# A hybrid attention and retention step on one core: sampled values' products one pair later, the last gate's first two pairs in one group, sampled output turned in parts

## What is computed

```python
u = rms_norm(h, g_pre)
z = einsum('bsd,de->bse', u, w_in)             # 22528 columns: q, k, v, gates of both branches
ya = dilated window attention(q, k, v) * silu(za)      # 3 groups of 8 heads, head size 128
yr = retention(q, k, v, state), normed * g_ret * silu(zr)   # 8 heads, 256 x 256 state
merged = sigmoid(ga) * (ya @ w_a_out) + sigmoid(gb) * (yr @ w_r_out)
h = h + rms_norm(merged @ w_o, g_post)
h = h + sigmoid(h @ w_ple_gate) * (p @ w_ple_proj)
```

## Time and profile before

| | |
|---|---|
| median of 3 runs | 2968.15 us (2966.22 to 2971.32) |
| profiled execution, its own time | 2968.77 us |
| its span, first to last instruction | 2967.0 us |
| mean granted TensorE clock | 0.99 |
| busy: PE, DVE, ACT, POOL | 98%, 59%, 38%, 12% of the span |
| DMA | 567.16 MB, mean 191 GB/s |

### The profile page before, as it was taken

The page is one execution under the profiler, slowest core; times in us unless marked ns, Lnnn a source line. Parts: engine busy times, 40 slices in busy tenths (PEclk is TensorE's granted clock), DMA queues, the critical chain, the costliest instruction groups (busy, mean ns, idle before and its releaser), DMA issues.

```text
span 2967.0 us, 57337 instructions
## 1 busy us (share of the span) xinstructions
PE 2901.2 (98%) x23566; PEld 2860.4 (96%) x23566; DVE 1762.1 (59%) x3199; ACT 1142.2 (38%) x2078; POOL 350.6 (12%) x517
## 2 busy tenths in 40 slices
PE   7999999999999999999999999999999999999898
PEld 7999999999999998999999999999999999999898
DVE  6766766656666656566666666666654433434632
ACT  5444434444443433433333434344443322334332
POOL 2010000100001011112112112110001101001200
PEclk9999999999999999999999999999999999999999
DMA  8465655656656545456456456476668656553442
GB/s 269 133 219 170 196 184 182 197 172 192 198 172 198 171 146 191 143 189 217 139 196 220 136 199 220 160 270 239 224 220 314 241 193 212 218 191 116 170 156 72
DMA packets 377942, 567.16 MB, mean 191 GB/s; under 512 B 16136, under 2 KB 340552, under 8 KB 374472
## 3 DMA queue, kind: packets, MB, share of 16 engines
q1 hardware_dynamic: 336448, 428.32, 42.0%
q0 software_dynamic: 41232, 135.17, 14.6%
HBM read 511.42 MB, written 228.16 MB: 249 GB/s over the span
## 4 chain that ended last, share of the span: by engine, by line
PE 86%; DMA 5%; DVE 5%; DVEq 1%; ACT 1%; issue 1%; SPq 0%; POOL 0%; ACTq 0%; POOLq 0%
PE acc L536 55%; PE acc L548 21%; DMA raw_weights<-in_w_in 3%; DVE weights L1340 1%; PE aux L746 1%; PE aux L757 1%; PE aux L767 1%; PE aux L834 1%; PE aux L641 1%; PE aux L824 1%; ACT weights L964 1%; DMA stage_buffers<-in_x_prompt 1%; PE aux L702 0%; PE aux L649 0%; PE aux L671 0%
## 5 line engine op out<-in xcount | busy, mean ns | idle before, releaser
L536 PE MATMUL acc<-moving,weights 128*128 128x260 f32 x12384 | 1578.2, 285 | 0.0
L536 PEld LDWEIGHTS acc<-moving,weights 128*128 128x128 f32 x12384 | 1520.8, 189 | 7.6 <-issue 4.0
L1340 DVE TENSOR_TENSOR weights<-raw_weights,weights 128x512 fp32r<-128x512 f32 (+1 forms) x1030 | 709.8, 694 | 601.9 <-ACT weights L964 565.5
L964 ACT ACTIVATE weights<-raw_weights 128x512 fp32r<-128x512 f32 (+1 forms) x1030 | 641.1, 626 | 1070.8 <-PE acc L536 472.2
L548 PE MATMUL acc<-moving,weights 128*128 128x260 f32 x5760 | 702.7, 284 | 15.0 <-DVE moving L1912 7.9
L548 PEld LDWEIGHTS acc<-moving,weights 128*128 128x128 f32 x5760 | 697.9, 190 | 16.7 <-DVE moving L1912 9.1
L536 PE MATMUL acc<-combined_moving,weights 128*128 128x260 f32 x3096 | 423.1, 286 | 0.0
L536 PEld LDWEIGHTS acc<-combined_moving,weights 128*128 128x128 f32 x3096 | 390.3, 189 | 0.5
L1415 DVE SCALAR_TENSOR_TENSOR stage_buffers<-acc,partial_sums 128x260 f32<-128x260 f32 x344 | 146.6, 478 | 180.2 <-PE acc L536 180.2
L964 ACT ACTIVATE weights<-combined_weights 128x512 fp32r<-128x512 f32 x172 | 108.0, 628 | 332.6 <-PE acc L536 314.3
L1340 DVE TENSOR_TENSOR weights<-combined_weights,weights 128x512 fp32r<-128x512 f32 x172 | 118.5, 689 | 144.0 <-ACT weights L964 143.1
(11 more groups left out here) (259 smaller groups left out, 1784.6 us busy)
## 6 DMA issues: line engine op xcount, KB each, us to landing
out<-in_cache_win SPq DMA_DIRECT2D x128, 1023.5 KB, 8.5
raw_weights<-in_w_in SPq DMA_DIRECT2D x96, 1024.0 KB, 5.8
raw_weights<-in_w_in SPq DMA_DIRECT2D x160, 512.0 KB, 5.2
out<-in_cache_win SPq DMA_DIRECT2D x32, 1022.0 KB, 9.3
out<-stage_buffers POOLq DMA_DIRECT2D x120, 256.0 KB, 3.0
stage_buffers<-in_cache_win POOLq DMA_DIRECT2D x48, 512.0 KB, 5.6
stage_buffers<-in_state_ret POOLq DMA_DIRECT2D x64, 256.0 KB, 6.2
raw_weights<-in_w_r_out SPq DMA_DIRECT2D x16, 1024.0 KB, 5.5
```

The lines of the kernel that those rows point to most:

```text
L536: mm = pe.matmul(acc[:, m, half, 0:HC], W[:, g % AHEAD, wp, kk, :], mov(up, kk), start=(start and kk == 0 and n == 0), stop=(stop and kk = ...
L964: act.activation(W[:, g % AHEAD, 0, 0:src.shape[1]], src, ACT.Copy).then_inc(s_whi, 1)
L1340: dve.tensor_tensor(W[:, g % AHEAD, 1, 0:src.shape[1]], src, W[:, g % AHEAD, 0, 0:src.shape[1]].bitcast(F32), ALU.subtract).then_inc(s_wre ...
```

## The change

Three things are changed.

1. **Sampled parts of the retention stage.** On PE `sample_values` goes from block 9 of pair 0 to block 1 of pair 1 (from head 3 on, and in the first merge-gate pairs), with DVE's `sample_output` from pair 0 block 10 to pair 1 block 3. At head 1 `sample_scores` goes from block 8 to 10 of pair 0, `sample_probs` from block 4 to 7 of pair 1, with the softmax hooks of DVE and ACT moved to pair 1, blocks 1, 2 and 3, and `sample_weights` to block 9. On DVE the third `sample_states` of a head goes from block 1 to block 0 of pair 2.
2. **Last gate.** The first two pairs get mode Q and run as one group (`first_four`): for every 4 k tiles all four output tiles, two in `acc`, two in the four banks of `aux`. A half of `raw` now holds 4 k tiles of all four output tiles. The later steps of the four tiles are moved behind, into pairs 1 and 2.
3. **Output.** The sampled columns are turned in four parts (pairs 3, 5, 7 and the end). POOL stores the last two tiles without waiting between them, and SP stores the sampled rows.

```diff
-       "L": [("raw", c, m) for c in range(4) for m in range(2)],
+       "Q": [("quad", c, t) for c in range(2) for t in range(4)],
...
-            add_pair("L" if w is w_gate and i == 0 else "N", w, (2 * i * P, 2 * i * P + P))
+            add_pair("Q" if w is w_gate and i < 2 else "N", w, (2 * i * P, 2 * i * P + P))
...
+            if p.mode == "Q":
+                r0 = ((p.nth - WG) * 2 + half) * 4 * P
+                sp.dma_start(raw[:, half].rearrange("p (k a) m c -> p k (a m c)", a=2),
+                             p.w[0][r0:r0 + 4 * P, 0:4 * P].rearrange("(k p) c -> p k c", p=P)).then_inc(s_wload[half], 16)
+                return
...
         sp.wait_ge(s_copy, 16 * N_COPIES)
+        sp.wait_ge(s_osrow, 1)
+        sp.dma_start(y_sample.rearrange("b o (q c) -> (b o) q c", q=4), osr[0:NS, :, 0:T]).then_inc(s_osst, 16)
...
-                attention_tail if h == 0 else {1: [ret_norm], 7: [ret_spread], **({8: [sample_scores]} if h == 1 else {}),
-                                               **({9: [sample_values]} if h >= 3 else {})},
-                {4: [sample_probs]} if h == 1 else {},
+                attention_tail if h == 0 else {1: [ret_norm], 7: [ret_spread], **({10: [sample_scores]} if h == 1 else {}),
+                                               },
+                {7: [sample_probs]} if h == 1 else {1: [sample_values]} if h >= 3 else {},
...
+        def first_four():
+            for t in range(2):
+                acc_ready(t)
+            for b in range(4):
+                pe.wait_ge(s_free[b], count.due(s_free[b]))
+            for part_of in range(2):
+                p = pairs[WG + part_of]
+                for n in range(p.n):
+                    c, t = divmod(n, 4)
+                    pe.wait_ge(s_wready, p.first + n + 1)
+                    for kk in range(4):
+                        k = 8 * part_of + 4 * c + kk
+                        if t == 0:
+                            pe.wait_ge(s_mov, 3 * KD + H + k + 1)
...
-            plain_pair(pairs[WG + i], {2: [lambda: out_turn(0)], 6: [lambda: out_turn(1)]} if i else {},
...
+        first_four()
+        for i in range(2, KD // 2):
+            mine = {2: [lambda: out_turn(0)], 6: [lambda: out_turn(1)]} if i > 2 else {
+                1: [lambda: out_turn(0)], 2: [lambda: out_turn(1)], 4: [lambda: out_turn(0)], 6: [lambda: out_turn(1)]}
+            if i in (3, 5, 7):
+                mine[4] = [lambda: sample_out_turn(i // 2 - 1)]
+            plain_pair(pairs[WG + i], mine)
...
-                    (1, 6): [lambda: sample_states(1, h)], (2, 0): [lambda: sample_ret_y(1, h)],
-                    (2, 1): [lambda: sample_states(2, h)], (2, 7): [lambda: sample_ret_y(2, h)],
+                    (1, 6): [lambda: sample_states(1, h)], 
+                    (2, 0): [lambda: sample_ret_y(1, h), lambda: sample_states(2, h)], (2, 7): [lambda: sample_ret_y(2, h)],
...
+            if i == KD // 2 - 1:
+                pool.dma_start(dst, rows).then_inc(s_ost, 16)
+            else:
+                store(dst, rows, s_ost, s_ofree[j])
```

More of the change, by code:

```diff
@@ L413, in half_of @@
         op = OPS[p.mode][n]
-        return {"sum": None, "raw": op[1] // 2, "two": op[1]}[op[0]]
+        return {"sum": None, "raw": op[1] // 2, "two": op[1], "quad": op[1]}[op[0]]
     def halves_of(p):
@@ new lines, in sample_out_turn @@
+        def sample_out_turn(q):
+            bank = 2 + q % 2
+            pe.wait_ge(s_os, q + 1)
+            pe.wait_ge(s_free[bank], count.due(s_free[bank]))
+            for n in range(4):
+                mm = pe.transpose(aux[0:NS, bank, n * P:(n + 1) * P], outS[:, (4 * q + n) * NS:(4 * q + n + 1) * NS], ident[:])
+            mm.then_inc(s_full[bank], 1)
+            fills.add(f"sample out {q}", bank)
+        first_four()
[5 more added lines that the diff above has]
+            plain_pair(pairs[WG + i], mine)
@@ L935, in _ @@
         out_turn(0)
         out_turn(1)
[L937 to L944 removed]
+        sample_out_turn(3)
     @block.scalar
@@ L1300, in ple_out, with sample_rows_out @@
             act.drain().then_inc(s_onat, 1)
-        def ple_gate(p, j):
-            act.wait_ge(s_used, p.first + (4 * (j + 1) if p.mode == "N" else 7 + j))
-            if p.nth > WG or j:
-                act.wait_ge(s_out, 2 * (p.nth - WG) + j)
-            act.activation(halves(sgt), acc[:, j, :, 0:HC], ACT.Sigmoid).then_inc(s_accfree[j], 1)
+        def sample_rows_out(q):
+            bank = 2 + q % 2
+            act.wait_ge(s_full[bank], filled.due(f"sample out {q}"))
+            act.activation(osr[0:NS, q, 0:T], aux[0:NS, bank, :], ACT.Copy).then_inc(s_free[bank], 1)
@@ new lines, in ple_gate @@
+        def ple_gate(t):
+            i, j = divmod(t, 2)
+            act.wait_ge(s_used, pairs[WG + i].first + 4 * (j + 1) if i > 1 else pairs[WG + 1].first + 5 + t)
+            if t:
+                act.wait_ge(s_out, t)
+            if i == 1:
+                act.activation(halves(sgt), aux[:, 2 * j:2 * j + 2, 0:HC], ACT.Sigmoid).then_inc(s_free[2 * j], 1)
+                act.drain().then_inc(s_free[2 * j + 1], 1)
+            else:
+                act.activation(halves(sgt), acc[:, j, :, 0:HC], ACT.Sigmoid).then_inc(s_accfree[j], 1)
@@ L1313, in _ @@
         ple_out(0)
         ple_out(1)
-        act.wait_ge(s_os, 1)
-        for q in range(4):
-            act.wait_ge(s_full[q], filled.due(f"sample out {q}"))
-            a = act.activation(osr[0:NS, q, 0:T], aux[0:NS, q, :], ACT.Copy)
-        a.then_inc(s_osrow, 1)
+        sample_rows_out(3)
+        act.drain().then_inc(s_osrow, 1)
     @block.vector
```

72 lines of the change are left out of this document (43 added, 29 removed).

## The result

| | before | changed |
|---|---|---|
| median | 2968.10 us (2966.22 to 2971.32) | 2927.94 us (2926.46 to 2929.35) |
| ratio | | 0.9868, 95% interval 0.9855 to 0.9881 |
| profiled execution, span | 2968.77, 2967.0 us | 2926.46, 2924.6 us |
| mean granted clock | 0.99 | 0.996 |

A fourth execution of the changed kernel took 4048 us at a mean clock of 0.651; it is left out of the range and the ratio, but the median has it (without it: 2926.54 us). A second set of runs of the same kernel gave 2928.58 us against 2968.61, ratio 0.9865 (0.9849 to 0.9881).

A forecast was written before the change was run, and what follows sets the result against it. PE, busy 98% of the span, was taken as the bound, leaving its idle time and slow clock to win. Retention 21.6, gate 3.8 and end 5.1 sum to 30.5 us off 2968.8: 2938 us, range 2932 to 2951.

The forecast's parts named there:

- The values, 14.0: Sampled values, line 824: 6.3 us idle, 6.5 slow clock behind it and 1.2 in the line itself go.
- first rival: The clock is not given back, since one-column products stay: 12.6 us of clock terms lost, 2951 us; chance 0.16.
- The wait of line 746 stays: At the scaled keys' product PE's 5.6 us of waits remain, since the same DVE work stands ahead.
- the later values' load: POOL gets its value buffer back some 7.4 us later, about covered by slack; costed at 0, bounds 0 and -2.
- The clock, 12.6: Slow clock regained in the retention stage: 7.7 us at the values, 2.4 at the scores, 2.5 at the probabilities.
- Deductions of 2.0 for new waits and for the probabilities: Retention stage: 1.0 us for DVE's lateness met by PE elsewhere, 1.0 for part of the probabilities' wait staying.
- 21.6: Retention stage's forecast gain in us: values 14.0, DVE's lateness -1.0, scores 5.2, probabilities 3.4.
- The gate, 3.8: Last gate's start: group of four gains 5.9 us, three turns cost 1.3, a clock fall 0.8; net 3.8.
- The end, 5.1: Output: last store issued 5.0 us earlier, by SP with POOL not waiting; gain 5.1 us, bounds 2.9 and 5.8.
- The second: Last gate: group of four does nothing, as later users of its tiles hold the blocks; 5.9 us lost, 2944; chance 0.12.
- The third: Everything goes: no probabilities wait, DVE lateness or gate clock fall, one state's wait less; 4.6 us more, 2933; chance 0.06.
- The fourth: Slower: POOL's later loads delay `scaled_states` and ACT's weights, PE starves at six heads; 39 us lost, 2977; chance 0.03.

The follow-up runs named there:

- all three retention edits: The kernel before with sampled values, scores and probabilities, and DVE's third states' step moved, last gate and output as before: 2937.55 and 2940.54 us.

## Why the prediction was right and wrong

- **The values, 14.0.** Near in size: alone they gave 15 to 17, as the last of three 13.5. The waits and the low clock at their places went as forecast. What I had taken for the cause of the low clock, the long wait together with the products, is right only in part: I had not looked up the wait ahead of the slow matmuls at 1355, which is 0.50 us, so "the fall came behind the long waits" (first rival) was a misreading.
- **"The wait of line 746 stays".** This step failed: 3.9 us went there (5.6 to 1.7), 3.2 of them from head 3 on, where the values are moved. The reason given, that the same DVE work stands ahead, was right for the states' step, which indeed gives nothing. But I had costed the later values' load as a loss or nothing (0 to -2), when the earlier load was costing time: cutting that load alone gave 9 us in the kernel before, and 2.5 to 3 in the changed one. The states' waits (line 834, 2.5 us in two) went as well; I had taken up only the waits of lines that the edit names.
- **The clock, 12.6.** Mis-sized; the windows give 17.2 between 1100 and 2050. I took the excess from the durations of single groups of matmuls. That fell short in three places: of head 1's fall (6.9 us in the windows from 1120 to 1160) I had 4.9, of the values' (8.5) I had 7.7, and the fall behind the states' wait at 1384 (1.7) was not in the list at all.
- **Deductions of 2.0 for new waits and for the probabilities.** The probabilities have no wait. DVE's lateness did come back, but as 2.7 us in place of 1.0: 1.65 ahead of the values at 1564, 0.26 at 1890, and 0.8 for a partial sum at head 1.
- Together: 5.7 us too little idle (3.9 at the keys, 2.5 at the states, 1.0 for the probabilities, less 1.7 more of new waits) and 4.6 too little clock. That is 10.3 of the 10.6 us between 21.6 and 32.2, and the miss of the total (40.2 by the medians against 30.5).
- **The gate, 3.8.** Right in size and in order (4.3 by the milestones): waits of 1.7, 2.4 and 0.7 us were worked out from DVE's rows, the profile has 1.57, 2.17 and 0.47, and the group took 51.4 us where 51 were expected. Of the clock I had set aside 0.8: it is lost in some executions (a window of 0.83 in the second profile of the changed kernel) and not in others.
- **The end, 5.1.** 5.6 in the profile: behind ACT's last tile copy the issue comes 4.9 us earlier, as forecast (5.0), and the stretch from the issue to the span's end is 0.8 us shorter, where I had put 0.1.
- **The rivals.** The first, that the clock is not given back, is refuted: no window between 1100 and 2050 is below 1.00 in the changed kernel. The second, that the group gives nothing, is refuted by 4.3 us. The third, that everything goes, was the nearest but was priced at 4.6 us beyond the forecast, where 10 came. The fourth, that POOL's slip starves PE, had the sign wrong: PE waits for no `scaled_states` there, and the slip of the values' load is part of the gain, some 6 us by what cutting the load gives in the two kernels. On the clock the Trainium skill ("TensorE: Matmul & The Clock Gate") would leave the ramp out of such sums as below 1% of the span; here it was 17.2 us of 2967, 0.6%, within its bound, but two fifths of the change, so for a comparison of two versions it has to be in the sum.
- **The range** was built from the forecast's own deductions on one side. Since every wait that I knew of in the stage could go, the lower end had to be the sum of all its idle and clock, 36 us, and not 5 us below the likeliest value.

## What to carry to other kernels

Cost a move by the whole stage, not by its line: add up all idle and all clock lost in the stage where the moved work stands, ask for each wait whether the move relieves it, and put the total of them at the edge of the range. A transfer that starts later, because its buffer is freed later, can be a gain; look at what is issued within a microsecond or two of it. When a group of work is regrouped so that one input is needed half as often, work out at once when the other input is due, and place its preparation by that: here this gave another 3.6 us by the medians, for blocks prepared one to four tiles earlier.

## What was not expected of the hardware

- The same wait at the same place has the low clock behind it in one kernel and not in another: line 548 waited 1.96 us at 2264 in the kernel before with 1.00 in the windows around it, and 2.05 us at 2232 with all three retention edits with 0.83. Two executions of the changed kernel differ too (0.83 behind 2.07 us, 1.00 behind 1.61). What decides it no run here shows. These are the rows with all three edits:

```profile
2231.85 10.43 PE L548 MATMUL acc<-moving,weights 128*128 128x260 f32 x72 [2.05 <-DVE stage_buffers L1415]
```

```profile
2230.00:2240.00 10.00, 8.15 (x55) 8.19 (x56) 4.79 (x9) 3.92 (x8) 3.65 (x7) 0.83 1.02 393
```

- With these waits gone, the executions seem to agree better: 19 of the kernel before lie between 2961.9 and 2972.6 us, four of the one with all three edits, measured beside them, between 2936.6 and 2938.7. Four executions span less than nineteen by their number alone, so this is a hint only.
- One-column products bring the low clock without any idle time on PE, and the engine shows busy 10.00 in a window where it has two thirds of its speed.
